# Dense FFN of a two-layer decoder step: a third weight slot pair, another order for the first three column pairs, an earlier first token sum, and the down-weight sums on another engine

## The reference, cut to what matters

```python
def swiglu(x, w1, w3, w2):
    h = jax.nn.silu(jnp.einsum('btd,df->btf', x, w1)) * jnp.einsum('btd,df->btf', x, w3)
    return jnp.einsum('btf,fd->btd', h, w2)
# x: 288 x 1024, w1, w3: 1024 x 2816, w2: 2816 x 1024, all float32
# x <- LN(ALPHA*x + mix(x)); x <- LN(ALPHA*x + swiglu(x))
```

## Time and profile before

| | |
|---|---|
| median of three runs | 1071.86 us (1070.45 to 1076.71) |
| the profiled execution | 1070.19 us, span of its instructions 1068.4 us |
| PE busy | 1033.4 us, 97% of the span |
| DVE, ACT, POOL busy | 416.6, 181.8 and 181.7 us |
| up stage on PE | from 216 to 379 us of the span |
| down stage on PE | from 379 to 468 us |

### The profile page before, as it was taken

One profiled execution on the slowest core, in us unless ns is written; L12 is line 12 of the kernel. 1 busy time (PEld: TensorE's weight loads), 2 busy tenths in 40 slices (PEclk: granted clock), 3 DMA queues, 4 the chain that ended last, 5 costly groups with the idle time before them and its releaser, 6 DMA issues.

```text
span 1068.4 us, 22711 instructions
## 1 busy us (share of the span) xinstructions
PE 1033.4 (97%) x10345; PEld 773.7 (72%) x10345; DVE 416.6 (39%) x817; ACT 181.8 (17%) x393; POOL 181.7 (17%) x138
## 2 busy tenths in 40 slices
PE   8999999989999999999999999989999999999995
PEld 6787766989999999987877768634656656566542
DVE  5654635555434564248456352521011011010134
ACT  1332224031111100033232231500000000000011
POOL 1010123703876600000011110040000020000020
PEclk9999999999999999999999999989999999999998
DMA  9352239206444225204521439789999999998961
GB/s 343 130 197 80 79 102 336 94 1 267 159 158 158 80 109 205 97 8 152 198 79 44 138 91 377 287 276 394 422 397 412 411 399 408 424 422 356 419 236 50
DMA packets 36548, 240.17 MB, mean 225 GB/s; under 512 B 4768, under 2 KB 8096, under 8 KB 16736
## 3 DMA queue, kind: packets, MB, share of 16 engines
q1 hardware_dynamic: 26896, 216.40, 51.8%
q0 software_dynamic: 6416, 19.52, 5.2%
q10 hardware_dynamic: 3136, 2.75, 0.8%
HBM read 228.60 MB, written 13.07 MB: 226 GB/s over the span
## 4 chain that ended last, share of the span: by engine, by line
PE 89%; DVE 4%; DMA 3%; issue 1%; ACT 1%; POOL 0%; SPq 0%; another core or an unknown queue 0%; DVEq 0%; POOLq 0%
PE ps L660 73%; PE ps L1160 12%; PE ps L1252 3%; DMA up_slots<-in_ffn_w 3%; PE ps L663 1%; DMA up_slots<-in_w_in 1%; DVE overlay L1923 1%; DVE x L1928 0%; SPq L414 0%; ACT overlay L1554 0%; ACT x L1554 0%; DVE up_slots L2342 0%; POOL up_slots L559 0%; DVE tables L2561 0%
## 5 line engine op out<-in xcount | busy, mean ns | idle before, releaser
L660 PE MATMUL ps<-up_slots,mix_or_moe 128*32 128x352 f32 (+2 forms) x3248 | 249.2, 455 | 5.7 <-DVE mix_or_moe L2606 3.6
L660 PE MATMUL ps<-x,up_slots 128*128 128x288 f32 (+2 forms) x944 | 233.8, 400 | 1.6 <-DMA up_slots<-in_w_in 1.6
L660 PEld LDWEIGHTS ps<-up_slots,mix_or_moe 128*32 128x32 f32 (+2 forms) x3248 | 123.6, 112 | 123.0 <-issue 33.3
L660 PEld LDWEIGHTS ps<-x,up_slots 128*128 128x128 f32 x944 | 169.2, 190 | 51.6 <-issue 8.3
L660 PE MATMUL ps<-overlay,tables 128*32 128x256 f32 (+4 forms) x2020 | 126.7, 375 | 0.3 <-ACT overlay L1554 0.3
L660 PEld LDWEIGHTS ps<-overlay,tables 128*32 128x32 f32 (+2 forms) x2020 | 88.3, 114 | 35.6 <-issue 3.4
L1160 PE MATMUL ps<-overlay,up_slots 128*128 128x144 f32 x704 | 93.8, 290 | 6.1 <-DVE overlay L2406 2.4
L1160 PEld LDWEIGHTS ps<-overlay,up_slots 128*128 128x128 f32 x704 | 90.0, 193 | 7.3 <-issue 5.1
L2600 DVE TENSOR_TENSOR mix_or_moe<-mix_or_moe,ps 128x352 f32<-128x352 f32 x24 | 11.3, 518 | 197.9 <-PE ps L660 191.1
L660 PE MATMUL ps<-overlay,up_slots 128*128 128x128 f32 (+3 forms) x560 | 86.0, 314 | 1.0 <-ACT overlay L1554 1.0
L660 PEld LDWEIGHTS ps<-overlay,up_slots 128*128 128x128 f32 x560 | 78.0, 191 | 8.6 <-ACT overlay L1554 1.9
(11 more groups left out here) (325 smaller groups left out, 995.6 us busy)
## 6 DMA issues: line engine op xcount, KB each, us to landing
up_slots<-in_moe_w SPq DMA_DIRECT2D x64, 1408.0 KB, 14.4
overlay<-in_moe_w SPq DMA_DIRECT2D x21, 1536.0 KB, 13.1
up_slots<-in_ffn_w SPq DMA_DIRECT2D x30, 1024.0 KB, 6.9
up_slots<-in_w_in SPq DMA_DIRECT2D x27, 1024.0 KB, 4.9
up_slots<-in_w_out SPq DMA_DIRECT2D x8, 1024.0 KB, 9.3
overlay<-in_moe_w SPq DMA_DIRECT2D x7, 1024.0 KB, 15.4
mix_or_moe<-in_states POOLq DMA_DIRECT2D x6, 512.0 KB, 10.6
out_sample_states<-mix_or_moe POOLq DMA_DIRECT2D x6, 512.0 KB, 6.0
```

Of the source, the lines that this page charges most:

```text
L660: return pe.matmul(o, lhsT, rhs, start=start, stop=stop)
```

## The change

- Pairs 0 to 7 go round three slot pairs, (0, 1), (6, 7), (2, 3); pairs 8 to 10 use (0, 1) and (6, 7). SP issues pair 2 after the second output panel's products, pair n from 3 to 7 after `up_ps` n - 2, pairs 8 to 10 after n - 1 as before; `down_in(0)` moves behind pair 7.
- The POOL weight sums of pair n no longer wait for `up_ps` n - 1 but for the three products p5, p6 and p3 of pair n - 2, one by one.
- PE and ACT take the steps of pairs 0 to 2 in an interleaved order. The sum with `S5B` gets a name, `c22`, and the next `s5` waits for it and not for `c21`. `c12` comes early for pair 2 too.
- In the layer norm's second half DVE scales six tiles, makes t1 once `x_ready` is 12, and then scales the last two tiles.
- `down_weight_sum` moves from DVE to POOL, behind the last `weight_sum`; panel 0's sums wait for `up_ps` 10, those of later panels for the products of the panel before that read the same buffers.

```diff
-UP_SLOTS = ((0, 1), (6, 7))
+UP_SLOTS = [((0, 1), (6, 7), (2, 3))[n % 3] if n < 8 else ((0, 1), (6, 7))[n % 2] for n in range(NUP)]
...
+FFN_START = "p1_0 p1_1 p2_0 p2_1 p5_0 p6_0 p3_0 p7_0 p5_1 p4_0 p3_1 p6_1 p1_2 p7_1 p5_2 p4_1 p2_2 p6_2 p3_2 p7_2 p1_3 p4_2 p5_3 p6_3 p2_3 p7_3 p3_3 p4_3"
+FFN_ACT_START = "s1_0 s1_1 s5_0 g11_0 g11_1 s5_1 silu_0 s1_2 s5_2 silu_1 g11_2 s1_3 silu_2 s5_3 g11_3 silu_3"
...
-                    for n in range(11):
+                    for n in range(NUP):
                         if n == 1:
                             sp.wait_ge(*mark("mixed", "B", 0))
-                        elif n > 1:
-                            sp.wait_ge(S["up_ps"], n - 1)
-                        if n == 3:
-                            down_in(0)
+                        elif n == 2:
+                            sp.wait_ge(S["out_ps"], 2)
+                        elif n > 2:
+                            sp.wait_ge(S["up_ps"], n - 2 if n < 8 else n - 1)
...
+                        if n == 7:
+                            sp.wait_ge(S["up_ps"], 6)
+                            down_in(0)
...
                     pool.tensor_tensor(s1, a21, a22, ALU.add).then_inc(S["w_sums"], 1)
                 if i == 1:
                     pool.wait_ge(S["w_sums"], 4 * n + 1)
+                    if n >= 2:
+                        pool.wait_ge(*ffn("ffn_pe", "p6", n - 2))
...
+            def down_weight_sum(m, i):
+                w = WD[m % 2]
+                s1, s2, s4 = (DNSUM[:, k] for k in range(3))
+                a11, a12, a21, a22 = (w[:, k::2, b:b + P] for b in (0, P) for k in range(2))
+                if i == 0:
+                    if m == 0:
+                        pool.wait_ge(S["up_ps"], NUP - 1)
+                    else:
+                        pool.wait_ge(*ffn("ffn_pe", "d5", m - 1))
+                    for j, s in enumerate(DOWN_SLOTS[m % 2]):
+                        pool.wait_ge(full[s], loaded["down", m, j])
+                    pool.tensor_tensor(s1, a21, a22, ALU.add).then_inc(S["dw_sums"], 1)
...
                     for n in range(NUP):
-                        if n >= 2:
-                            pool.wait_ge(S["up_ps"], n - 1)
                         for i in range(4):
                             weight_sum(n, i)
+                    for m in range(3):
+                        for i in range(4):
+                            down_weight_sum(m, i)
...
-                    scale(0, 0, 1, "ln_mix_g")
+                    rstd(0, 1)
+                    scale_tiles(0, 0, 1, "ln_mix_g", range(6))
...
+                    v.wait_ge(S["x_ready"], KT + KH)
+                    tt(t1, x12, x11, SU).then_inc(S["x_sums"], 1)
+                    scale_tiles(0, 0, 1, "ln_mix_g", range(6, KT))
...
-                        later_sum(n, 0)
                         v.wait_ge(*ffn("ffn_ac", "g11", n))
...
-                        tt(CB[:, :, 2], CB[:, :, 2], S5B, AD)
+                        ffn_done(tt(CB[:, :, 2], CB[:, :, 2], S5B, AD), "ffn_dv", "c22", n)
...
-                        if m < 2:
-                            down_weight_sum(m + 1, 0)
```

More of the change, by code:

```diff
@@ L111 @@
 STEPS = {name: steps.split() for name, steps in STEPS.items()}
+FFN_START = "p1_0 p1_1 p2_0 p2_1 p5_0 p6_0 p3_0 p7_0 p5_1 p4_0 p3_1 p6_1 p1_2 p7_1 p5_2 p4_1 p2_2 p6_2 p3_2 p7_2 p1_3 p4_2 p5_3 p6_3 p2_3 p7_3 p3_3 p4_3"
+FFN_ACT_START = "s1_0 s1_1 s5_0 g11_0 g11_1 s5_1 silu_0 s1_2 s5_2 silu_1 g11_2 s1_3 silu_2 s5_3 g11_3 silu_3"
+FFN_PRODUCTS, FFN_ACT_STEPS = ([(s.split("_")[0], int(s.split("_")[1])) for s in text.split()] for text in (FFN_START, FFN_ACT_START))
+FFN_PRODUCTS += [(p, n) for n in range(4, NUP) for p in ("p1", "p5", "p6", "p2", "p7", "p3", "p4")]
+FFN_ACT_STEPS += [(a, n) for n in range(4, NUP) for a in ("s1", "s5", "g11", "silu")]
 FFN = {
[L115 to L116 removed]
+    "ffn_pe": [step for step in FFN_PRODUCTS if step[0] != "p4"]
     + [(p, m) for m in range(3) for p in ("d1", "d5", "d6", "d2", "d7", "d3")],
     "ffn_dv": [(v, n) for n in range(NUP)
[L119 removed]
+               for v in (("u2", "c12", "h11", "u3", "c22", "c21") if n < 3 else ("u2", "h11", "u3", "c12", "c22", "c21"))]
     + [(v, m) for m in range(3) for v in ("ds1", "ds5", "du2", "du3")],
[L121 to L122 removed]
+    "ffn_ac": FFN_ACT_STEPS,
 }
@@ L1234, in _ @@
                     up_p2(1)
[L1235 to L1241, removed]
-                            up_p1(n)
[L1243 to L1247, removed]
+                    up_p5(0)
+                    up_p6(0)
+                    up_p3(0)
+                    up_p7(0)
+                    up_p5(1)
+                    up_p4(0)
+                    up_p3(1)
+                    up_p6(1)
+                    up_p1(2)
+                    up_p7(1)
+                    up_p5(2)
+                    up_p4(1)
+                    up_p2(2)
+                    up_p6(2)
+                    up_p3(2)
+                    up_p7(2)
+                    up_p1(3)
+                    up_p4(2)
+                    for n in range(3, NUP):
+                        if n > 3:
+                            up_p1(n)
+                        up_p5(n)
+                        up_p6(n)
+                        up_p2(n)
+                        up_p7(n)
+                        up_p3(n)
                         up_p4(n)
@@ L1753, in _, with up_s5, up_g11, up_silu @@
                 if l == 0:
-                    for n in range(NUP):
-                        if n >= 2:
-                            up_s1(n)
+                    def up_s5(n):
                         act.wait_ge(*ffn("ffn_pe", "p5", n))
                         if n:
-                            act.wait_ge(*ffn("ffn_dv", "c21", n - 1))
+                            act.wait_ge(*ffn("ffn_dv", "c22", n - 1))
                         ffn_done(f(S5B, PS[:, 6:8, 0:TH], ACT.Copy), "ffn_ac", "s5", n)
+                    def up_g11(n):
                         act.wait_ge(*ffn("ffn_pe", "p2", n))
                         ffn_done(f(hid[:, 2 * n, 0:TH], PS[:, 2 * (n % 2), 0:TH], ACT.Silu), "ffn_ac", "g11", n)
+                    def up_silu(n):
                         act.wait_ge(*ffn("ffn_dv", "c21", n))
@@ L1765, in _ @@
                         ffn_done(f(rest, CB[:, 0].rearrange("p a t -> p (a t)"), ACT.Silu), "ffn_ac", "silu", n)
+                    up_s5(0)
+                    up_g11(0)
+                    up_g11(1)
+                    up_s5(1)
+                    up_silu(0)
+                    up_s1(2)
+                    up_s5(2)
+                    up_silu(1)
+                    up_g11(2)
+                    up_s1(3)
+                    up_silu(2)
+                    for n in range(3, NUP):
+                        if n > 3:
+                            up_s1(n)
+                        up_s5(n)
+                        up_g11(n)
+                        up_silu(n)
                     sqrt_ready()
@@ L2388, in _ @@
                     fold_squares(0, 1)
-                    scale(0, 0, 1, "ln_mix_g")
+                    rstd(0, 1)
+                    scale_tiles(0, 0, 1, "ln_mix_g", range(6))
+                    x11, x12, x21, x22 = (X[:, k:k + KH, c] for k in (0, KH) for c in (first, second))
+                    t1, t2, t3, t4 = (TU[:, i] for i in range(4))
+                    v.wait_ge(S["x_ready"], KT + KH)
+                    tt(t1, x12, x11, SU).then_inc(S["x_sums"], 1)
+                    scale_tiles(0, 0, 1, "ln_mix_g", range(6, KT))
                 else:
@@ L2403, in _ @@
                     v.wait_ge(S["x_ready"], 2 * KT)
-                    x11, x12, x21, x22 = (X[:, k:k + KH, c] for k in (0, KH) for c in (first, second))
-                    t1, t2, t3, t4 = (TU[:, i] for i in range(4))
-                    sig(tt(t1, x12, x11, SU), S["x_sums"], 1)
+                    v.wait_ge(S["x_sums"], 1)
                     sig(tt(t2, x22, t1, SU), S["x_sums"], 2)
```

60 lines of the change are left out of this document (24 added, 36 removed).

## The result

The changed kernel takes 1080.52 us (median of 16 runs, 1076.82 to 1089.09) where the kernel before took 1070.87 beside it (16 runs, 1068.04 to 1076.71). The ratio is 1.0098, with a 95% interval of 1.0082 to 1.0114: slower by about 1%, 10.5 us. Forecast were 1077.4 us, a range of 1064 to 1083, and "slower" as the likeliest of three.

A forecast was written before the change was run, and what follows sets the result against it. PE, busy for 97% of the span, was taken as the bound. The terms -1.3 - 0.7 - 0.9 - 2.35 + 7.8 + 3.0 gave +5.55 us on 1071.86, which is 1077.4 us, with a range of 1064 to 1083.

The forecast's parts named there:

- Down sums of panel 0: End of the up stage: POOL's sums hold DVE's hidden sums, so PE stops ahead of p7(10); +7.8 us.
- second rival: Ahead of p7(10): a late landing leaves only two POOL sums in between; +5.1 us there, 1074.7 us in all; chance 0.20.
- third rival: Ahead of p7(10): four POOL sums, as hidden sum 4 doesn't slip in; +10.9 us there, 1080.5 us in all; chance 0.17.
- Clock after that stop: Behind the stop ahead of p7(10): PE's clock falls to half pace, as after an earlier long gap; +3.0 us.
- p7(4): Up stage: the wait forecast ahead of p7(2) comes again a pair later, ahead of p7(4); about 0.5 us.
- p7(2): Up stage: POOL's sums of pair 3 hold DVE's steps, so PE waits 2.5 us where there was 0.70.
- Clock at 230: PE's half-speed stretch of 1.75 us behind the gap at p5(0): half taken as won; -0.9 us.
- First token sum: Start of the up stage: t1 runs earlier, so p5(0) starts at about 227.8 in place of 229.06; -1.3 us.
- The two waits of 0.64, and 1.26 and 0.45: PE's gaps ahead of p4(0) and p4(1), and of p5(3) and p6(3): all go with interleaving and third slot.
- Down stage: DVE no longer waits for loads in the midst of its queue, so PE's two waits go; -2.35 us.
- first rival: Ahead of p7(10): DVE passes group 4's hidden sums through one break between POOL sums; faster, 1066.6 us; chance 0.25.
- The fourth: Up stage: the third slot brings nothing by itself; already in the forecast as the new wait at p7(2), no own chance.

The follow-up runs named there:

- first run: The changed kernel with one more wait: POOL begins panel 0's down-weight sums only after DVE's u2 of pair 10; ratio 1.001, stage 250.93 us.
- ninth run: The kernel before with the down-weight sums moved to POOL, panel 0's held until after DVE's u2(10); ratio 0.9986, stage 242.61 us.
- third run: The kernel before with only the down-weight sums moved to POOL, behind the last up-weight sum; ratio 1.0074, stage 252.89 us.
- fourth run: The changed kernel with each of POOL's four sums of down panel 0 cut into two instructions; ratio 1.0031, stage 247.58 us.
- eighth run: The changed kernel with all down-weight sums on DVE as before, and POOL's sums of pair n from 3 on begun after u2(n - 1); ratio 0.9959, stage 237.75 us.

## Why the prediction was right, and which terms were off

- **The mechanism** held in every point that was tried: DVE's two-input sums and POOL's sums take turns by whole instructions, and the stop sits ahead of p7(10). The stop was undone by one wait (first, ninth run), made alone (third), and cut from 6.97 to 2.43 us by halving the instructions, each hidden sum being held about half as long (fourth).
- **Down sums of panel 0**: +7.8 forecast, 6.97 idle measured, inside 4.7 to 10.9. Three POOL sums lay in between, as in the forecast, but by another road, and that is luck. Pair 10's first sum began at 361.80, 7.6 us behind p4(8) at 354.17 and not 7.45. So line 2449's step (now 2499) just got in ahead of POOL's last up sum, hidden sum 1 came right behind that sum as in the second rival, and sum 4 didn't slip in, as in the third: one hold less and one more. The 3.1 us taken for a POOL sum of 1408 elements was 3.16 where nothing held it.
- **Clock after that stop**: +3.0 forecast, 2.60 measured. The stretch it was taken from was read too long: 0.50 held from about 697.6 to 704.4 us (the 0.81 and 0.78 of the earlier trace rows at its ends), so PE worked 5.5 us in it and lost 2.8.
- **p7(4)** is the term that was mis-sized: +0.5 forecast, +5.44 measured and 2.5 of half speed behind it, for which the sum had no term at all. Together that is 7.5 us more than forecast. I let hidden sums 2 to 4 run freely once pair 5's sums were done. But in the new order only 11.8 us lie between the ends of p4(2) and p4(3), so pair 6's load landed just then, and its sums held hidden sums 3 and 4 for one POOL sum each. I had looked for back-to-back POOL work only at pair 10, while the third slot made it in the early pairs too. The first run shows the same thing one pair earlier.
- **p7(2)**: 2.5 forecast, 1.90 measured there, 2.04 to 7.47 in the other runs with this order and no rest.
- **Clock at 230**: -0.9 forecast; the stretch went from t1 and came back behind p7(2), so the net was 0.
- **First token sum** -1.3 forecast, -1.23 measured (gap 2.41 to 1.18). **The two waits of 0.64, and 1.26 and 0.45**: gone as forecast. **Down stage**: -2.35 forecast, both waits gone.
- The forecast sum, 5.55 us, was about half of the 10.5 measured. The stop at p7(4) was 7.5 us too low and the clock at 230 another 0.9; panel 0's stop, the clock behind it and p7(2) came out smaller than forecast and took back 1.8. The measured 1080.5 is the very time of the third rival, (c), but by chance: not four POOL sums but three lay ahead of u2(10), and the rest came from p7(4).
- What it named as able to prove it wrong, several two-input DVE steps getting through between two POOL sums that follow each other at once, was seen nowhere: in this stage of all fourteen traces some 300 such steps began while a POOL sum ran, and every one ended behind that sum's end.
- The first rival (hidden sums get past) fell. Hidden sums did pass freely where POOL rested, as forecast: 2 to 4 of group 0 took 0.46 us each between 256.0 and 257.4. The fourth, that the third slot brings nothing by itself, holds in the form in which it was changed, and not once POOL rests.

## What to carry to other kernels

Before moving work to GpSimd, list the DVE instructions with two SBUF inputs that the busiest engine waits for, and count them against GpSimd instructions, one for one: each can wait for a whole one, however short it is. A load, slot or wait that lets GpSimd start earlier can cost more than it wins (here about 8 us of the stage); tie the start of its batch to the DVE step behind the sensitive ones, or cut its instructions smaller. An engine that idles in a regular pattern may be what keeps another on time.

## What the runs showed of the hardware that was not expected

- DVE's steps with two SBUF inputs and POOL's sums take strict turns even when a DVE instruction is queued right behind another without a wait (3.29 and 3.40 us, one POOL sum each). DVE steps with one PSUM input stay at 0.30 to 0.46 us throughout. A three-operand step with two tensors in SBUF (the first run's down stage) took 3.19 us behind a POOL sum in place of 0.30.
- The clock after a gap is not settled by the gap's length near 2 us: 2.41 and 2.40 us at t1 were followed by 0.50 (kernel before, third run), 2.41 in the ninth run was not; 2.12 and 2.43 in the fourth run were not, 1.90 and 2.04 ahead of p7(2) were. In this stage none of the gaps up to 1.73 us was (1.73 in the eighth run, 1.59 in the kernel before), and all seven from 3.14 to 7.47 us were. Why the middle ones differ stays open.
